# Hybrid attention block on one core: the sliding branch's mask and maximum in one VectorE operation, with an earlier exponential and a rewoven start and end

## The reference

```python
def _hybrid_layer(x, mem, cos, sin, g_in, w_in, attn_sinks, g_mem, w_mem_kv, w_branch, w_out):
    h = _rmsnorm(x, g_in)
    proj = h @ w_in                       # split into the branches' parts and the gates
    ...
    y_a = _sliding_window_sink_attention(a_q, a_k, a_v, attn_sinks)        # 8 heads of 64
    y_b = _dsa_sparse_attention(b_q, b_k, b_v, b_qi, b_ki, b_wi)           # top 256 keys
    y_c = _memory_cross_attention(c_q, m_k, m_v)                           # 4 heads of 128, 256 keys
    ys = jnp.stack([y_a * silu(a_z), y_b * silu(b_z), y_c * silu(c_z)], axis=2)
    u = jnp.einsum('bsnc,ncd->bsnd', ys, w_branch)
    merged = jnp.sum(sigmoid(gates) * u, axis=2)
    return x + merged @ w_out             # and a final RMSNorm

# sliding window: queries of a chunk of 64 tokens see that chunk and the one before it,
# and a sink per head stands in the softmax's sum
scores = jnp.where(valid, q @ k * dh ** -0.5, MASK_VALUE)
p = softmax(concatenate([scores, sink], axis=-1))[..., :-1]
```

## Time and profile before

| | before |
|---|---|
| median of 3 runs | 2812.31 us (2811.92 to 2814.73) |
| profiled execution | 2818.59 us, span 2816.8 us |
| mean granted TensorE clock in it | 0.972 of full |
| TensorE busy | 2528.1 us, 90% of the span |
| VectorE, ScalarE, GpSimd busy | 1786.0, 1372.1, 410.3 us |

### The profile page before, as it was taken

How to read it: one execution, slowest core, us unless ns; L and a number is a source line. 1 busy time by engine, 2 the same in 40 slices (tenths; PEclk the granted TensorE clock), 3 DMA queues, 4 the chain that set the end, 5 groups by cost and what they waited for, 6 DMA issues and landing times.

```text
span 2816.8 us, 37280 instructions
## 1 busy us (share of the span) xinstructions
PE 2528.1 (90%) x13093; PEld 2095.4 (74%) x13093; DVE 1786.0 (63%) x3597; ACT 1372.1 (49%) x2768; POOL 410.3 (15%) x397
## 2 busy tenths in 40 slices
PE   5998999998999999999898999999878888878896
PEld 4776888776778888877677778887667777667785
DVE  6466676225767687227778878622778887777522
ACT  4455645344646444216657445522665673454511
POOL 5334353440000000100000000010000001000010
PEclk9999999999999999999999999999999999999998
DMA  5756584785343522664343511166324333000154
GB/s 162 227 176 213 170 282 150 252 278 183 115 162 119 173 76 68 209 209 155 115 143 104 165 60 53 46 217 206 137 83 149 105 108 132 23 31 31 38 179 165
DMA packets 172537, 399.36 MB, mean 142 GB/s; under 512 B 13760, under 2 KB 96704, under 8 KB 162368
## 3 DMA queue, kind: packets, MB, share of 16 engines
q1 hardware_dynamic: 172352, 396.96, 42.8%
HBM read 308.31 MB, written 88.60 MB: 141 GB/s over the span
## 4 chain that ended last, share of the span: by engine, by line
PE 51%; DVE 21%; ACT 15%; issue 10%; DMA 1%; POOL 1%; SPq 0%; DVEq 0%; ACTq 0%; POOLq 0%
PE bank L861 38%; PE TR L760 5%; PE PV L828 5%; ACT signs L1026 4%; ACT prob L991 3%; ACT prob L1001 3%; DVE ptL L1396 2%; ACT ptH L1015 2%; DVE prob L1355 2%; DVE nmx L1365 2%; DVE score L1617 2%; DVE zs L1427 1%; PE bank L771 1%; PE bank L772 1%; DVE flags L1543 1%
## 5 line engine op out<-in xcount | busy, mean ns | idle before, releaser
L861 PE MATMUL bank<-hH,pairs 128*128 128x512 f32 (+1 forms) x3584 | 1158.5, 393 | 21.0 <-DVE zs L1459 7.6
L861 PEld LDWEIGHTS bank<-hH,pairs 128*128 128x128 f32 x3584 | 679.3, 191 | 160.6 <-issue 22.2
L861 PE MATMUL bank<-hL,pairs 128*128 128x512 f32 (+2 forms) x1792 | 704.1, 393 | 0.0
L1026 ACT ACTIVATE signs<-score,bits 128x384 int8<-128x384 f32 (+7 forms) x256 | 335.8, 1312 | 214.5 <-DVE bits L1497 201.5
L1396 DVE TENSOR_TENSOR ptL<-TR,ptH 128x512 fp32r<-128x512 f32 (+1 forms) x384 | 256.9, 670 | 260.1 <-ACT ptH L1015 256.9
L861 PEld LDWEIGHTS bank<-hL,pairs 128*128 128x128 f32 (+1 forms) x1792 | 343.3, 192 | 65.2
L1015 ACT ACTIVATE ptH<-TR 128x512 fp32r<-128x512 f32 (+1 forms) x384 | 219.6, 576 | 333.6 <-PE TR L760 332.6
L1478 DVE TENSOR_SCALAR_CACHE_REDUCE above<-score,bits 128x256 uint8<-128x256 f32 (+10 forms) x280 | 348.1, 1243 | 9.5
L760 PE MATMUL TR<-identR,prob 128*128 128x128 f32 x1480 | 232.6, 279 | 101.0 <-ACT prob L1001 53.2
L760 PEld LDWEIGHTS TR<-identR,prob 128*128 128x128 f32 x1480 | 178.1, 142 | 178.4 <-ACT prob L1001 66.9
L1176 POOL TENSOR_TENSOR pairs<-raw,pairs 128x512 fp32r<-128x512 f32 x164 | 218.1, 1339 | 316.1 <-ACT pairs L960 315.9
(11 more groups left out here) (206 smaller groups left out, 3636.1 us busy)
## 6 DMA issues: line engine op xcount, KB each, us to landing
pairs<-w_split SPq DMA_DIRECT2D x444, 512.0 KB, 3.5
w_split<-pairs SPq DMA_DIRECT2D x74, 1024.0 KB, 4.9
raw<-in_w_in SPq DMA_DIRECT2D x106, 256.0 KB, 5.6
xs<-in_x SPq DMA_DIRECT2D x4, 2048.0 KB, 9.2
rows<-in_x SPq DMA_DIRECT2D x16, 512.0 KB, 5.2
out<-rows SPq DMA_DIRECT2D x4, 2048.0 KB, 7.5
table<-trig SPq DMA_DIRECT2D x48, 128.0 KB, 2.8
raw<-in_w_branch SPq DMA_DIRECT2D x24, 256.0 KB, 5.6
```

Source lines behind the costliest of these rows:

```text
L861: done = nc.tensor.matmul(PJ[st.u + half * up][0:min(st.width, P), 0:st.n_tok], lhs, rhs[:, row, 0:st.n_tok], start=(n % 12 == 0 and (up o ...
L1026: nc.scalar.activation(signs[:, 0:keys], score[:, tt, 0:keys], ACT.Sign, bias=thr.bitcast(F32)[:, tt:tt + 1], scale=-1.0, accum_out=cnt[:, ...
```

## The change

It has four parts. **Sliding scores:** the mask products on TensorE are gone; VectorE's `windowed` adds mask to scores, keeps the result in SBUF (`prob`) and takes each block's extremum, beginning with the sink's value, in one operation for each of the four blocks. The exponentials read `prob`, and the banks come free when `windowed` is done. **Exponentials' place:** `due` puts ScalarE's `exps` into half 0 for branches `a` and `c`. **End:** four of the last group's eight `finish` steps are woven between the last four `out` units; the others follow per tile with that tile's squares; and each tile is stored by its own DMA. **Start:** a dummy square makes ScalarE load its table early; the wait for the small inputs and the four weight splits stand behind the root.

```diff
@@ order_of_work
+    def finish_last(g):
+
+        for tt in range(NT):
+            finish(g, 2 * tt + 1, 2 * tt + 2)
+            steps.append(Step("row_squares", g=g, tr=n["tr"], tt=tt, tiles=1))
         steps.append(Step("row_scale", g=g, tr=n["tr"]))
...
-                    s_freed.append(event("dve_s") if branch == "b" else ("p_exp", n["e"] + len(it.chunks)))
+                    s_freed.append(event("dve_s") if branch != "c" else ("p_exp", n["e"] + len(it.chunks)))
...
+            if m == KC // 2 - 1:
+                half_out = last_out
             if g + 1 < NG and m < KC - 1:
                 norm("x", g + 1, m + (m > 0), m + 2)
-    finish(NG - 1)
-    finish_rows(NG - 1)
+            elif g + 1 == NG and m >= KC // 2:
+                first = 2 * (m - KC // 2)
+                steps.append(Step("finish", g=g, tr=take("tr"), i=first, evac=half_out.evac))
+    finish_last(NG - 1)
@@ due
             if st.branch != "b":
-                return [0 for _ in after], [ticks - 1]
+                return [0 for _ in after], [0]
@@ SyncE
+                        for t in range(NT):
+                            sp.wait_ge(S["out_ready"], NT * st.g + t + 1)
+                            sp.dma_start(out_v[st.g, :, t, :], rows[:, t, :]).then_inc(S["store"], 16)
@@ TensorE, scores of branch a
-                            nc.tensor.matmul(bank[:, o:o + 256], identR[:, :], wmask[:, 0 if g == 0 and tt == 0 else 1, :],
-                                             start=True, stop=False)
-                            nc.tensor.matmul(bank[:, o:o + 256], lhs, wkA[:, kv, keys], start=False, stop=False)
+                            nc.tensor.matmul(bank[:, o:o + 256], lhs, wkA[:, kv, keys], start=True, stop=False)
@@ ScalarE, exps
+                elif branch == "a":
+                    of = it.tt * 4
+                    for n, (_, first, size, s) in enumerate(it.chunks):
+                        act.wait_ge(S["dve_s"], s_freed[s][1])
+                        if n:
+                            act.wait_ge(S["p_sub"], it.m + 1)
+                            nc.scalar.activation(esnk[:, it.norm % 2, of:of + 4], snk[:, it.m % 2, :], ACT.Exp)
+                        for o in range(first, first + size, 256):
+                            part, i = held(it)[:, o:o + 256], o // 256
+                            last = nc.scalar.activation(part, part, ACT.Exp, bias=nmx[:, it.m % 2, i:i + 1], scale=-1.0,
+                                                        accum_out=sums[:, 0, of + i:of + i + 1])
+                        last.then_inc(S["p_exp"], 1)
@@ ScalarE, start
                     if st.source == "mem":
-                        act.wait_ge(S["small_in"], 16 * (NG + 3))
+                        act.wait_ge(S["consts"], 1)
+                        nc.scalar.activation(squared[:, 0:P], identR[:, :].bitcast(F32), ACT.Square).then_inc(S["squared"], 1)
...
                     squares(nt, tokens)
+                elif st.kind == "scale":
+                    n_root += 1
+                    root(n_root, 0, source_rows(st)[0])
                     if st.source == "mem":
+                        act.wait_ge(S["small_in"], 16 * (NG + 3))
                         for half in range(4):
                             split_hi(half // 2, half % 2)
@@ VectorE
+            def windowed(it, g):
+
+                a = it.m % 2
+                for _, c, size, s in it.chunks:
+                    dve.wait_ge(S["s_full"], s + 1)
+                    for o in range(0, size, 256):
+                        i = (c + o) // 256
+                        head, tt = 2 * it.h + i // 2, 2 * it.tt + i % 2
+                        last = nc.vector.tensor_tensor_reduce(held(it)[:, c + o:c + o + 256], SC[s][:, o:o + 256],
+                                                              wmask[:, 0 if g == 0 and tt == 0 else 1, :].bitcast(F32),
+                                                              -HD ** -0.5, nsink[:, head:head + 1], ALU.add, ALU.min, nmx[:, a, i:i + 1])
+                    last.then_inc(S["dve_s"], 1)
+                dve.wait_ge(S["dve_s"], s_freed[s][1])
+                TT(snk[:, a, :].rearrange("p (e t) -> p e t", e=2), nmx[:, a, :].rearrange("p (e t) -> p e t", e=2),
+                   paired(sink[:, 2 * it.h:2 * it.h + 2], 2), ALU.add).then_inc(S["p_sub"], 1)
...
-                    link(STT(two, two, -HD ** -0.5, paired(nsink[:, 2 * it.h:2 * it.h + 2], 2), ALU.mult, ALU.min))
-                    TT(snk[:, a, :].rearrange("p (e t) -> p e t", e=2), two, paired(sink[:, 2 * it.h:2 * it.h + 2], 2),
-                       ALU.add).then_inc(S["p_sub"], 1)
```

More of the change, by code:

```diff
@@ L65, in __init__ @@
                  wt=None, u=None, evac=None, used=None, f=None, x=None, y=None, k=None, a=None, tr=None,
-                 p=None, pv=None, scale=None, norm=None, before=None, slots=None, behind=None, woven=None, ring=None):
+                 p=None, pv=None, scale=None, norm=None, before=None, tiles=None, slots=None, behind=None, woven=None, ring=None):
         self.kind = kind
@@ L73, in __init__ @@
         self.tr, self.p, self.pv, self.before, self.slots, self.behind = tr, p, pv, before, slots, behind
+        self.tiles = tiles
         self.scale, self.norm, self.woven, self.ring = scale, norm, woven, ring
@@ L962, in _, with squares @@
             n_squares = [0]
-            def squares(tiles, src):
-                for t in range(tiles):
+            def squares(tiles, src, first=0):
+                for t in range(first, first + tiles):
                     if n_squares[0]:
@@ L971, in squares, with root @@
                                          accum_out=ssq[:, t:t + 1]).then_inc(S["squared"], 1)
-            def root(n, tiles):
+            def root(n, first, tiles):
                 act.wait_ge(S["var_ready"], n)
-                nc.scalar.activation(rstd[:, 0:tiles], var[:, 0:tiles], ACT.Sqrt).then_inc(S["rooted"], 1)
+                nc.scalar.activation(rstd[:, first:first + tiles], var[:, first:first + tiles], ACT.Sqrt).then_inc(S["rooted"], 1)
             def exps(it, branch, head=0):
@@ L1154, in _ @@
                     act.wait_ge(S["tr_free"], st.tr)
-                    squares(NT, rows)
+                    squares(st.tiles, rows, st.tt)
                 elif st.kind == "row_scale":
                     n_root += 1
-                    root(n_root, NT)
+                    root(n_root, 0, NT)
         @block.gpsimd
@@ L1648, in _ @@
                             masked(items[0], n)
+                    elif branch == "a":
+                        windowed(items[0], st.g)
                     else:
-                        maxima(items[0], branch)
+                        maxima(items[0])
                     aside(st, (-1, 0))
@@ L1663, in _ @@
                                         masked(items[i + 1], n)
+                                elif here and branch == "a":
+                                    windowed(items[i + 1], st.g)
                                 elif here:
-                                    maxima(items[i + 1], branch)
+                                    maxima(items[i + 1])
                             beside(it, j)
```

32 lines of the change are left out of this document (12 added, 20 removed).

## The result

| | before | changed |
|---|---|---|
| median | 2812.11 us (2811.84 to 2814.73, 4 runs) | 2833.06 us (2830.70 to 2835.31, 4 runs) |
| ratio | | 1.0072, 95% interval 1.0055 to 1.0090 |
| profiled execution | 2818.59 us, span 2816.8 | 2830.70 us, span 2828.9 |
| TensorE, VectorE, ScalarE busy | 2528.1, 1786.0, 1372.1 us | 2528.9, 1793.6, 1380.2 us |
| mean granted clock | 0.972 | 0.967 |

The changed kernel is slower by 20.2 us (15 to 25), where +8.0 was forecast, and 2833 lies above the range of 2805 to 2829. The direction was right. TensorE's busy time did not fall although 128 products were gone: those it has left took longer, at a lower clock.

What follows compares the result with a forecast made beforehand. The prediction took the ScalarE-VectorE cycle to bound both attentions, and TensorE the stages between. Its terms, +21.2-1.7-4.2-7.3 = +8.0 us, gave a median of 2820.3 us, with a range of 2805 to 2829.

Steps and rivals of the forecast that it cites:

- Memory attention, +21.2: Memory attention: the second ptH queues behind the early exponentials, so signs starts later in each item; +21.2 us over four groups.
- Sliding attention, -1.7: Sliding attention: slightly longer items against earlier first and last items of each stage; -1.7 us, from -9 to +5.
- Items, +5.6: Sliding attention: half 0 longer, half 1 shorter, +0.2 us per item, times 7 items times 4 groups; +5.6 us.
- The stages' ends, -4.4: Last sliding item: its exponentials no longer follow the seventh's second ptH, so transposes and products come earlier; -4.4 us.
- The starts, -2.9: Sliding stages' beginnings: no mask products and exponentials startable after the first bank, so first transposes come earlier; -2.9 us.
- The start, -4.2: Kernel start: early table load and squares give scaled memory rows sooner to TensorE's first units; -4.2 us (-2.5 to -4.8).
- The end, -7.3: Kernel end: woven rounds let squares start earlier, and per-tile stores leave less behind the last; -7.3 us (-4 to -8).
- the stores' term: Within the end: only 512 KB remain behind the last store, landing in 3.6 to 4 us instead of 7.5; -3.3 us.
- TensorE bounds sliding attention: Rival, sliding attention: mask products lie on the cycle, so their 15 us come off; -5.3 in all, 2807.0 us; chance 0.12.
- memory attention's shift is hidden: Rival, memory attention: TensorE's woven units cover the delay, so that term is near 0; 2799.1 us; chance 0.08.
- the parts cancel: Case, whole kernel: end and start give all, memory term half; within 5.6 us of before; chance 0.08.
- More is lost: Rival, whole kernel: longer waits lower TensorE's clock, or windowed takes 0.6 per operation; 2828 to 2836 us; chance 0.14.

Runs made afterwards that it cites:

- the one with the cycle shortened: Kernel before with the three small operations for the next threshold directly behind ptL, ahead of zs and maxima, in sliding attention: 0.9911, -25.0 us.

## Why the prediction was wrong, step by step

**What bounds the kernel** was read rightly. In both attentions the cycle of ScalarE and VectorE sets the item. In sliding attention the run with the bits moved shows it, by taking 25 us off without touching a product; in memory attention the run with the exponentials early shows it, since a delay put on that cycle comes out in full. That TensorE stands before an item's first product for `zs` was true of groups 2 and 3 alone; in groups 0 and 1 of the profile before it never waited for `zs` in that stage, and the delay came out all the same.

**Memory attention, +21.2:** right in mechanism and size. Alone it is +21.9; items are longer by 2.3 and 1.8 as worked out (10.88 for 8.58 and 10.39 for 8.57 above), 2.8 in group 0.

**Sliding attention, -1.7:** the step that failed; it holds 10 of the 12 us by which the forecast missed. It measured +8.4. Of its three terms one was mis-sized, one did not come, and one came. *Items, +5.6:* in the run of the part alone the stages from first `ptH` to last are 2.9, 2.2, 1.6 and 2.3 us longer, +9.0. The item of the earlier trace rows is longer by the +0.2 that I took, but others are longer by up to 0.6, and two items of group 0 by 0.7: their half 1 gives nothing back (2.61 us for 2.64). I let one item stand for 28; what makes the others longer by more than 0.2 isn't shown. For the two of group 0 the changed profile's timelines of VectorE and GpSimd show it, here in the fourth item:

```profile
313.26 0.69 DVE L1428 TENSOR_TENSOR ptL<-TR,ptH 128x512 fp32r<-128x512 f32 x1 [3.32 <-ACT ptH L1035]
313.87 0.87 DVE L1517 TENSOR_TENSOR bits<-small 128x4 int32<-128x4 f32 x1
...
315.18 0.48 DVE L1510 TENSOR_SCALAR_CACHE_REDUCE above<-score,bits 128x256 uint8<-128x256 f32 x1
...
312.23 2.49 POOL L1199 TENSOR_TENSOR pairs<-raw,pairs 128x512 fp32r<-128x512 f32 x2 [4.78 <-ACT pairs L970]
```

The first of the three small operations, 0.15 us elsewhere, took 0.87, and it ended with GpSimd's pair of splits. Before the change it did the same, 0.92 us, but mostly beneath the exponentials (2.64 us for the 2.37 of other halves); with these gone from half 1 it stands on the cycle. The page "SBUF — State Buffer" of the Trainium skill, section "SBUF: two separate sides", has a VectorE operation with two SBUF inputs and a GpSimd operation that reads SBUF take a shared port pair in turns, each for a whole instruction; the rows agree (VectorE's ends at 314.74, GpSimd's at 314.72).

*The stages' ends, -4.4:* I priced how much earlier TensorE's transposes of the last item could come, because TensorE stands before them. But the `ptH` that wants them stands in ScalarE's queue behind `signs`; it comes when the cycle comes. From the last item's first `ptH` to its second both profiles run alike, 5.0, 5.4, 6.2 and 7.1 us by group in each. From there to the first `ptH` of top-k attention the run of the part alone is 0.1 us longer, 0.8 shorter, 0.4 and 1.0 longer: in sum no gain. *The starts, -2.9,* came. In the run of the part alone the first transposes follow the first product of the scores 0.9, 0.5, 0.8 and 0.8 us sooner. In the changed kernel's profile group 0 lost 0.6 instead: TensorE's products followed one another at 0.42 us instead of 0.23 for the first 3.4 us, at a granted clock of 0.57 from 261 to 265 us, where it was 1.00 in the same place before. So one term took an item for all items, and another took an engine's wait for a gain without asking whether the consumer was free.

Half 0 of the item, 5.18 us, fell on the upper end of my 4.96 to 5.17 by luck. I had `signs` wait for the bits there, and my own 1.64 us for 1.56 makes them only 0.1 later; the run with the mask alone shows 0.09. The other 0.67 are the exponentials, behind which `signs` stands in its queue. And 0.4 per item gives +3.9 us for the part, not the +5 of the upper bound.

What I had not priced at all is the slower exponential: reading SBUF, the exponentials pace at 0.50 instead of 0.45 us, 0.2 per item, which in half 1 lies on the cycle. In the change their place moved too; the run that leaves them in half 1 shows it.

**The start, -4.2:** -4.8 alone, with 4.5 us at the first transpose in that run's profile and 5.9 in the changed kernel's; the table load ran at 0.7, before any data.

**The end, -7.3:** right in its steps, -10.4 alone (interval to -6) and -13.8 with the start, for the -11.5 of both. Both figures of the stores' term were too long: the last store had landed 6.6 us after issue in the profile before, not the 7.5 of the other three, and 512 KB land after 2.8 where I had taken 3.6 to 4. The difference, 3.6 for my 3.3, held all the same. Why the time gained 10.4 where the profiles show 7.4 isn't settled; the interval holds both. The page "DMA: Bandwidth & Descriptors" of the Trainium skill, section "Anatomy of one DMA", gives a fixed 2.0 us and 1.2 us for these bytes, 3.2 by its estimate, for DMAs that GpSimd issues; these are SyncE's. 2.8 is near that, and what I feared from it, that four pay in series, did not come.

**The rivals.** That TensorE bounds sliding attention fell for this kernel, and came near to true in groups 0 and 1 of the one with the cycle shortened, where the mask products are worth 3.4 and 3.3 us. That memory attention's shift is hidden fell, and so did that the parts cancel. *More is lost* named the range in which the time came out, 2828 to 2836, but for other causes: `windowed` is 0.476 us, pace 0.41, not 0.6, and memory attention costs 21.9 us for 21.2 although the clock is lower there (see below).

**The baseline.** The time before was 2812.3 in three runs; the kernel before had 2814.3 to 2814.8 as its median in 42 further runs, from 2809.5 to 2820.6. Its spread, in code that did not change, is as wide as the parts that were to be summed. Against these runs the changed kernel's 2833.06 is 18.3 to 18.8 us slower, which leaves some 2 us between it and the parts' +16.5.

## What to carry to other kernels

An early place in a queue is paid by what is queued behind it: price a moved instruction by its wait, not its duration, and follow the instruction that it overtakes through to the next engine. A wait of an engine is worth its length only if what it delays is what the next one is waiting for, so name the consumer's own queue before taking the gain. And where two engines hand a small result to and fro, look for the long operation that stands ahead of that small one for no reason of data: here moving three operations of 0.2 us took 25 us off, where the four parts of the change together added 20.

## What the runs showed of the hardware

An exponential of 128x256 is issued every 0.45 us when it reads PSUM (L1001, mean 474 ns) and every 0.50 when it reads SBUF (L1012, 498 ns), with the same shape and accumulation; the second form works in place.

The mask's operation, which reads one PSUM and one SBUF operand and writes SBUF, takes 476 ns for 128x256 with a column as its start, of which 0.41 show in the pace; the same without a column was 418.

TensorE's granted clock fell in other places than before. Two stretches of top-k attention in group 3, whose code is the same in both kernels, in the profile before and in the one after (us, busy time and instructions of each engine, clock, DMA share, GB/s):

```profile
2400.00:2440.00 40.00, 33.01 (x222) 28.52 (x221) 30.67 (x73) 19.14 (x49) 0.61 (x1) 1.00 0.08 27
2480.00:2520.00 40.00, 32.35 (x217) 27.76 (x216) 31.35 (x70) 19.87 (x49) 1.89 (x2) 1.00 0.08 27
```

```profile
2416.00:2457.00 41.00, 34.02 (x206) 29.30 (x205) 29.65 (x70) 18.55 (x48) 0.61 (x1) 0.92 0.08 27
2498.00:2538.00 40.00, 32.35 (x204) 27.60 (x203) 30.09 (x65) 18.47 (x47) 1.90 (x2) 0.96 0.08 27
```

At 1.00 TensorE had 2.4 GHz throughout, at 0.92 it had 1.2 GHz for a part. That whole attention took 4 us longer in the changed kernel. In both it waits now and then for the exponentials there; nothing in the rows tells why the lower level was granted in one and not in the other, and the timed parts add up without it, so it stands here as variation and not as a cause.

In the edited stages the clock is lower with the edit. Over memory attention it was 1.00, 1.00, 0.94 and 0.92 by group before and 0.94, 0.95, 0.85 and 0.87 with the exponentials early there alone, where TensorE waits up to 2.8 us for `ptL`; over sliding attention of group 2 it was 1.00 before and 0.93 with the sliding part alone. The timed parts show no loss beyond what the longer items give, so what this costs by itself isn't told.
